# Tile-wise expert choice, split last output product and pre-weighted expert rows in a hybrid MoE layer

## The reference

```python
g_val, g_idx = lax.top_k(g_logits, 1)
...
e_val, e_idx = lax.top_k(e_in, TOP_K)
w_sel = jax.nn.softmax(e_val, axis=-1) * p_group
...
for e in range(N_EXPERTS):
    he = jax.nn.silu(h @ w_gate[e]) * (h @ w_up[e])
    y = y + combine[:, e:e + 1] * (he @ w_down[e])
```

## Time and profile before

| | |
|---|---|
| median of three runs | 708.25 us |
| the profiled execution | 710.35 us |
| its span | 708.4 us |
| TensorE busy | 693.4 us (98%) |
| VectorE busy | 294.6 us (42%) |
| HBM traffic over the span | 261 GB/s |

### The profile page before, as it was taken

The page is one execution under the profiler, slowest core; times in us unless marked ns, Lnnn a source line. Parts: engine busy times, 40 slices in busy tenths (PEclk is TensorE's granted clock), DMA queues, the critical chain, the costliest instruction groups (busy, mean ns, idle before and its releaser), DMA issues.

```text
span 708.4 us, 8000 instructions
## 1 busy us (share of the span) xinstructions
PE 693.4 (98%) x3274; PEld 417.6 (59%) x3274; DVE 294.6 (42%) x505; ACT 114.7 (16%) x199; POOL 180.9 (26%) x128
## 2 busy tenths in 40 slices
PE   9999999999999999999999999999999999999994
PEld 5444587555776457777877888647434434443431
DVE  3438492678320385744343324326413212212315
ACT  4111011111010422221122240013000000000004
POOL 0008989798369100710000000000000000000013
PEclk9999999999999999999999999998999999999997
DMA  8994536752433331533471235997999999999992
GB/s 354 420 396 186 183 145 237 297 201 96 179 114 124 118 115 33 209 120 118 176 297 61 76 148 207 426 392 296 374 418 421 420 423 420 421 420 421 418 408 81
DMA packets 29509, 183.70 MB, mean 259 GB/s; under 512 B 3543, under 2 KB 5975, under 8 KB 14624
## 3 DMA queue, kind: packets, MB, share of 16 engines
q1 hardware_dynamic: 27600, 178.98, 63.7%
q0 software_dynamic: 1584, 3.97, 1.4%
q10 hardware_dynamic: 288, 0.23, 0.1%
HBM read 178.14 MB, written 6.82 MB: 261 GB/s over the span
## 4 chain that ended last, share of the span: by engine, by line
PE 93%; DMA 2%; DVE 2%; POOL 1%; issue 0%; ACT 0%; DVEq 0%; POOLq 0%; ACTq 0%
PE bank L1183 21%; PE bank L798 18%; PE bank L802 10%; PE bank L794 8%; PE bank L815 6%; PE bank L1143 4%; PE bank L1021 4%; PE bank L821 4%; PE bank L946 2%; PE bank L967 2%; PE bank L844 2%; PE bank L808 2%; PE bank L954 2%; DMA y_rows<-sb,token_rows 1%; DMA sb<-y_rows 1%; PE bank L1000 1%
## 5 line engine op out<-in xcount | busy, mean ns | idle before, releaser
L1183 PE MATMUL bank<-sb 128*64 128x512 f32 x768 | 166.8, 593 | 0.7 <-ACT sb L729 0.7
L798 PE MATMUL bank<-sb 128*128 128x256 f32 x576 | 128.1, 381 | 0.0
L798 PEld LDWEIGHTS bank<-sb 128*128 128x128 f32 x576 | 108.2, 190 | 16.4 <-issue 2.4
L1183 PEld LDWEIGHTS bank<-sb 128*64 128x64 f32 x768 | 53.9, 137 | 106.9 <-issue 105.0
L584 POOL DMA_INDIRECT y_rows<-sb,token_rows x7 | 7.0, 1000 | 363.8 <-DVE sb L1740 363.8
L544 POOL TENSOR_TENSOR sb<-sb 128x1024 f32<-128x1024 f32 x32 | 66.8, 2089 | 55.6 <-DMA sb<-ada_w 36.0
L802 PE MATMUL bank<-sb 128*128 128x512 f32 x160 | 70.1, 593 | 0.0
L1372 DVE COPY sb<-bank 128x512 f32<-128x512 f32 x45 | 29.2, 685 | 96.4 <-PE bank L954 57.8
L794 PE MATMUL bank<-sb 128*128 128x512 f32 x128 | 55.8, 592 | 0.0
L802 PEld LDWEIGHTS bank<-sb 128*128 128x128 f32 x160 | 29.9, 190 | 34.7 <-issue 34.6
L1705 DVE TENSOR_TENSOR sb<-sb,bank 128x512 f32<-128x512 f32 x8 | 5.5, 688 | 97.1 <-PE bank L1183 97.1
(11 more groups left out here) (246 smaller groups left out, 689.8 us busy)
## 6 DMA issues: line engine op xcount, KB each, us to landing
sb<-expert_w SPq DMA_DIRECT2D x90, 1024.0 KB, 19.3
sb<-front_w SPq DMA_DIRECT2D x19, 2048.0 KB, 7.9
sb<-ada_w SPq DMA_DIRECT2D x32, 512.0 KB, 3.4
sb<-ada_mix SPq DMA_DIRECT2D x4, 2048.0 KB, 19.8
sb<-expert_w SPq DMA_DIRECT2D x12, 512.0 KB, 10.9
sb<-xcT SPq DMA_DIRECT2D x4, 512.0 KB, 6.3
sb<-front_w SPq DMA_DIRECT2D x4, 512.0 KB, 21.2
y_rows<-sb SPq DMA_DIRECT2D x4, 512.0 KB, 23.2
```

What stands on the lines that cost most here:

```text
L798: ins = pe.matmul(ps[:, c * L:(c + 1) * L], lhs(w, k, (2 * i + c) * P), hT[:, k, 0:L], start=(k == 0), stop=(k == KD - 1))
L1183: ins = pe.matmul(bank[e * CAP:(e + 1) * CAP, :], lhsT[:, k, e * CAP:(e + 1) * CAP], weights_at(k, e), start=(k == 0), stop=(k == parts - 1))
```

## The change

- The (out0, t1) product is cut after four of eight steps, tile zero is turned in between, and tile zero's router products and choice (`choose`, now for one tile) come before the end of the last output product. That product is made in two halves of 256 columns in different banks; residual, turning and routing of its tokens follow half by half.
- Positions, the first pair's one-hot matrix and the first gather are made tile by tile; `keep_warm` goes.
- `modulate` counts up after each block; the first gate product waits for one block at a time.
- The weight of each choice lies beside the token number, so that the product that finds a slot's row also finds its weight; `experts_out` multiplies it in before the rows are stored. Reads back are then plain adds; the weights' part of `choices` and ScalarE's two multiplications go. GpSimd's own reads are the first and the last of the four.
- VectorE adds both its rows before the last y, and the first scatter product before it waits for GpSimd. The multiplication by the gain moves to GpSimd. ScalarE issues the last output store.

The core of the diff (buffers, semaphores and renamed counters left out):

```diff
-        token_of = keep(NT * NE, NT, NE)
+        token_weight = keep(2 * NT * NE, NT, 2 * NE)
+        token_of, comb = [token_weight.rearrange("p t (e k) -> p t e k", k=2)[:, :, :, k] for k in range(2)]
...
-            sp.wait_ge(fill_ready, multiplied("out1"))
+            sp.wait_ge(last_out, 1)
             load_both(9)
...
-            for i in (1, 0):
-                for t in range(NT):
-                    cols = slice(512 * i, 512 * i + 512)
-                    sp.wait_ge(fin_by["act" if i == 0 else "dve"], t + 1)
-                    sp.dma_start(d["out"][t * P:t * P + P, cols], normed[:, t, cols]).then_inc(stored, 16)
+                                             .rearrange("a p n -> p (a n)")).then_inc(pass_in[m], 16)
+            for t, i in ((0, 1), (0, 0), (1, 1)):
+                cols = slice(512 * i, 512 * i + 512)
+                sp.wait_ge(fin_by["act" if i == 0 else "dve"], t + 1)
+                sp.dma_start(d["out"][t * P:t * P + P, cols], normed[:, t, cols]).then_inc(stored, 16)
             sp.wait_ge(stored, 16 * 2 * NT)
...
-            for q in range(2 * NT):
+            for q in (1, 0, NT, NT + 1):
                 pool.dma_start(y_back[:, q, :], d["y_rows"][q * P:q * P + P, :]).then_inc(y_in[q], 16)
             pool.wait_ge(acc_ready, 1)
...
-                pool.wait_ge(rows_weighted, q // NT + 1)
+                pool.wait_ge(y_in[q], 16)
                 pool.tensor_tensor(acc[:, 1, :], acc[:, 1, :], y_back[:, q, :], ALU.add).then_inc(pool_rows, 1)
                 pool.wait_ge(pool_rows, q // NT + 1)
+            pool.wait_ge(glast_in, 16)
+            for t in range(NT):
+                pool.wait_ge(scat_out, t + 1)
+                pool.tensor_tensor(xg[:, t, :], acc[:, t, 0:512], g_last[:, 0:512], ALU.mult).then_inc(xg_ready, 1)
...
-                    act.wait_ge(x1_ready, u + 1)
+                    act.wait_ge(x1_ready, u + 1 + (u == 3))
...
-            act.wait_ge(acc_ready, 1)
-            for q in (1, NT + 1):
-                act.wait_ge(y_in[q], 16)
-                act.activation(y_back[:, q, :], y_back[:, q, :], ACT.Copy, scale=slot_w[:, q:q + 1]).then_inc(rows_weighted, 1)
...
+            act.wait_ge(fin_by["act"], NT)
+            act.dma_start(d["out"][P:2 * P, 0:512], normed[:, 1, 0:512]).then_inc(stored, 16)
...
+                if ks[-1] < KD - 1:
+                    return
...
-            for n in range(first_out, first_out + 3):
+            for n in range(first_out, first_out + 2):
                 fill(n)
+            fill(first_out + 2, range(0, 4))
             turn_tokens(0, 0)
             turn_tokens(0, 1)
-            fill(first_out + 3)
+            fill(first_out + 2, range(4, KD))
+            route(0, 0)
+            route(0, 1)
+            def last_columns(p):
+
+                n = first_out + 3
+                ps = (banks[BANK_OF[n]], score[0])[p]
+                if p == 0:
+                    wait_emptied(pe, max(m for m in range(n) if BANK_OF[m] == BANK_OF[n]))
+                w = slot[SLOT_OF[FRONT.index("out1")]]
+                for k in range(KD):
+                    ins = pe.matmul(ps[:, 0:256], yT[:, k, P:2 * P], w[:, k * 512 + 256 * p:k * 512 + 256 * p + 256],
+                                    start=(k == 0), stop=(k == KD - 1))
+                ins.then_inc((fill_ready, last_out)[p], 1)
+
...
+                pe.wait_ge(x1_ready, 4 + p)
+                if p:
+                    pe.wait_ge(xT_out["act"], 1)
+                else:
+                    pe.wait_ge(xT_out["dve"], 2)
+                for c in range(2):
+                    k = 4 + 2 * p + c
+                    ins = pe.transpose(shared[1 - p][:, c * P:(c + 1) * P], x_nat[:, 1, k * P:(k + 1) * P], ident)
...
+                pe.wait_ge(xT_out["dve"], 3 + p)
+                for c in (2 * p, 2 * p + 1):
+                    ins = pe.matmul(route_bank[1][:, 0:ROUTES], xT[1][1][:, c, :], sm("router")[:, 4 + c, 0:ROUTES],
+                                    start=False, stop=(c == 3))
...
+            last_columns(0)
             turn_tokens(1, 0)
-            route(0, 0)
-            turn_tokens(1, 1)
-            route(0, 1)
+            pe.wait_ge(member_ready, 1)
+            pe.matmul(pv_bank[:, 256:272], sm("upto"), member[:, 0, :], start=True, stop=True).then_inc(pos_ready, 1)
+            last_columns(1)
+            turn_last(0)
             route(1, 0)
-            route(1, 1)
+            turn_last(1)
+            route_last(0)
+            route_last(1)
             for i, g in enumerate(POOLED[LOOP_SUMS:]):
                 pe.wait_ge(ada_summed, LOOP_SUMS + i + 1)
                 pe.matmul(banks[4 + i][:, :], ones, ada_sum[g], start=True, stop=True).then_inc(row5_ready, 1)
-            keep_warm(2)
...
+                for i in range(2):
+                    for c in range(4):
+                        ins = pe.matmul(banks[i][:, c * P:(c + 1) * P], x_nat[:, t, (4 * i + c) * P:(4 * i + c + 1) * P],
+                                        S_now[0][:, t, :], start=(t == 0 and c == 0), stop=(t == NT - 1 and c == 3))
+                    if t == NT - 1:
+                        ins.then_inc(gather_ready, 1)
...
+            pe.wait_ge(xn_first, 1)
+            pe.wait_ge(first_cut, 1)
+            gather_first(0)
+            pe.wait_ge(member_ready, 2)
+            pe.matmul(pv_bank[:, 272:288], sm("upto"), member[:, 1, :], start=True, stop=False)
...
             ins.then_inc(pos_ready, 1)
-            pe.wait_ge(xn_ready, NT)
+            pe.wait_ge(xn_ready, 1)
+            pe.wait_ge(cut_ready, 1)
+            gather_first(1)
...
-                    pe.wait_ge(h_out, 2 * n)
...
+                pe.wait_ge(choice_ready, 1)
...
-                    ins = pe.matmul(banks[7][:, 384 + 2 * n:386 + 2 * n], S[:, t, :], token_of[:, t, 2 * n:2 * n + 2],
+                    ins = pe.matmul(banks[7][:, 384 + 4 * n:388 + 4 * n], S[:, t, :], token_weight[:, t, 4 * n:4 * n + 4],
...
-                    if n is not None and k % 4 == 0:
-                        pe.wait_ge(h_out, 2 * n + (k // 4 + 1))
+                    if n is not None and q == 0:
+                        pe.wait_ge(h_out, k + 1)
+                    elif n is not None and k % 4 == 0:
+                        pe.wait_ge(h_out, KD * n + (k + 4))
...
-            gather(0, S_now[0])
...
-            residual(first_out + 2)
...
-            tokens_out(1, 1)
-            rstd(1)
-            dve.wait_ge(const_ready, 1)
-            logits(0)
-            link(logits(1))
-
+            residual(first_out + 2)
...
+            def choose(t):
+
...
+                link(dve.tensor_reduce(r_gm[:, col], g, AX.X, ALU.max))
+                first_best(r_sel[:, t, :], g, r_gm[:, col], sm("rank")[:, NE - NG:NE], r_t[:, t, :], r_sm[:, col])
...
+                first_best(oh2[:, t, :], em, r_m2[:, col], sm("rank"), r_et[:, t, :], r_sm[:, col])
+                dve.tensor_tensor(member[:, t, :], oh1[:, t, :], oh2[:, t, :], ALU.add).then_inc(member_ready, 1)
...
+                link(dve.tensor_tensor(posm[:, t, :], pv_bank[:, 256 + NE * t:256 + NE * t + NE], member[:, t, :], ALU.mult))
...
+                return dve.tensor_tensor(S_now[0][:, t, :].rearrange("p (e c) -> p e c", c=CAP),
+                                         slots_iota.unsqueeze(1).broadcast_to([P, 2, CAP]),
+                                         posm[:, t, 0:2].unsqueeze(2).broadcast_to([P, 2, CAP]), ALU.is_equal)
...
+            dve.wait_ge(const_ready, 1)
+            link(logits(0))
+            choose(0)
+            dve.tensor_scalar(x_nat[:, 0, :], x_nat[:, 0, :], x1_inv[:, 0:1], None, ALU.mult).then_inc(xn_first, 1)
+            positions(0)
+            cut_first(0).then_inc(first_cut, 1)
+            for p in range(2):
+                cols = slice(512 + 256 * p, 768 + 256 * p)
+                if p == 0:
+                    dve.wait_ge(fill_ready, len(FILLS))
+                else:
+                    dve.wait_ge(last_out, 1)
+                ps = (banks[BANK_OF[first_out + 3]], score[0])[p]
+                link(dve.tensor_tensor(spare[:, 1, cols], ps[:, 0:256], row2[:, cols], ALU.mult))
+                dve.tensor_tensor(x_nat[:, 1, cols], x_nat[:, 1, cols], spare[:, 1, cols], ALU.add).then_inc(x1_ready, 1)
+            for p in range(2):
+                dve.wait_ge(xT_ready, 4 + p)
+                dve.tensor_copy(xT[1][1][:, 2 * p:2 * p + 2, :].rearrange("p a b -> p (a b)"), shared[1 - p][:, 0:256])\
+                   .then_inc(xT_out["dve"], 1)
+            rstd(1)
+            link(logits(1))
+            choose(1)
+            dve.tensor_tensor(r_eg, r_all[:, :, 0:NG], wide(r_gm, NG), ALU.subtract).then_inc(gexp_in, 1)
             dve.tensor_tensor(r_d, r_m2, r_m1, ALU.subtract).then_inc(gexp_in, 1)
-            first_best(oh2, r_em, r_m2, sm("rank"), r_et, r_sm, NE)
-            dve.tensor_tensor(member, oh1, oh2, ALU.add).then_inc(member_ready, 1)
+            positions(1)
```

(38 more changed lines are left out.)

109 lines of the change are left out of this document (52 added, 57 removed).

## The result

The changed kernel takes **703.93 us** (703.33 to 705.02, 4 runs); the kernel before took 708.26 beside it (708.22 to 709.32, 4 runs). The ratio on record is 0.9921, 95% interval 0.9905 to 0.9937; it is not the quotient of these two medians, which is 0.994. It is faster, as forecast. But 700.4 was forecast, and 703.93 lies 0.7 above the range of 699.0 to 703.2; applied to the median of 708.25 the ratio gives 702.7 (701.5 to 703.8), which lies inside it. The profiled execution took 704.13, its span is 702.1.

What follows compares the result with a forecast made beforehand. Bounds: TensorE, busy 179.30 of 180.30 us during the experts, and chains of waits either side. Front 3.6 plus tail 4.25 gave 7.85: execution 710.35 to 702.5, less 2.1 to the median, 700.4 us; range 699.0 to 703.2.

Steps and rivals of the forecast that it cites:

- the signs named for being right: Among them: first gate product near 489.9, last load landing near 684, 9 to 10 us from last down product to end.
- The front's term: Ahead of the experts: the first gate product starts at 489.9 instead of 493.52, 3.6 us earlier.
- half a microsecond before TensorE asks: In the front: tile zero's choice, 3.2 us from 472.9, is made at 476.3, before TensorE wants it at 476.8.
- The loads' term: Weight loads: ninth pair waits 2.6 us longer, ring places free 3.6 earlier, 7.6 us unused; loads end 3 us earlier.
- The tail's term: Behind the experts: from the last down product to the span's end 9.6 us instead of 13.85, a gain of 4.25.
- E: The end of the last down product, from which the tail is counted; forecast at 690.95.
- The offset to the median: Profiled execution 710.35 lay 2.1 us above the runs' median 708.25; the forecast took this off, 702.5 to 700.4.
- The half clock: Rival, front: TensorE again granted 1.2 GHz around row sums and gathers, 3.4 us lost, part hidden; 702.9 us, chance 0.15.
- The reads did not land late: Rival, tail: loads end no earlier than 687.3, stored rows are read late; 702.5 or 703.4 us, chance 0.13.
- The first choice was early enough: Rival, front: both choices stand in series behind the last output product, 3.2 us more; 703.6 us, chance 0.07.
- Starving of weights: Rival, loads: delayed loads make TensorE wait; slower only if the last lands after 695.3; 9 later gives 709.2; chance 0.05.
- The port lock: Tail: GpSimd and two-SBUF-input VectorE adds exclude each other; late reads then come to 703.4 us, without it 702.5.

Runs made afterwards that it cites:

- short_ends: Changed kernel with one instruction fewer in each tile's choice, and GpSimd instead of ScalarE scaling tile zero's left half at the end; 704.32 us, 0.9916 of the kernel before.
- loads_later: Changed kernel, but the ninth pair of loads and all behind it also wait for the end of the router products; 705.12 us, 0.9947 of the kernel before.
- lock_free: Changed kernel with the final gains loaded after the third read of stored rows, and VectorE's last y before its second row add; 704.66 us, 0.9922 of the kernel before.
- before_again: The kernel before, unchanged, run and profiled once more; 709.74 us, 0.9996 of the kernel before.
- late_choice: Changed kernel, but tile zero's choice, scaling and cut stand just ahead of tile one's choice on VectorE; 708.21 us, 0.9988 of the kernel before.
- tail_only: Kernel before plus only rows weighted before storing, plain adds, gain on GpSimd and last store from ScalarE; 707.22 us, 0.9960 of the kernel before.
- before_no_warm: Kernel before without its two warm-up products ahead of the position product; 711.45 us, 1.0017 of the kernel before.

## Why the prediction was right and wrong

**The mechanism held.** By the stages the gate starts 2.97 earlier, the weighting on ScalarE is out of the chain, the clock stays at 1.00, and TensorE waits for no load inside a pair. How much of the 2.97 is the clock's and how much the earlier choice's was not separated: no profile shows the kernel before without the half clock. Of the signs named for being right, the gate (490.63), the last load (685.5) and the tail (10.46) each came short.

**The front's term, 3.6, measured 2.97.** What failed is the price of a choice: "16, so 3.2". It took 3.61, since an instruction on one tile costs nearly as much as one on two (0.17 on 16 columns, 0.19 on 32), and those with a scalar for each partition 0.23 and not 0.2. Twice 0.4 had been missed. The second shows in full. The first ate the cover of "half a microsecond before TensorE asks": TensorE was ready at 476.69, the choice came at 476.71, and the second half started some 0.2 late, as short_ends gave it back. Against the sum's own marks that half still ended near 480.5, because the work ahead of it was a little cheaper than summed; but the router products behind it ended at 483.26 and not 482.9, so that the second choice started at 483.64, 0.4 after the sum's 483.2. TensorE's wait ahead of the second choice's product, 0.45, stayed under the 0.5 that I had set as the mark of an error.

**The loads' term failed as a step.** "There is room for the first to vanish in the second": 6.0 of the unused 7.6 us lay from 485.7 on, around and behind the gate's start, and the earlier gate uses them up (404 GB/s and not 302). The later ninth pair opens a new hole ahead of it, 2.9 us at 23 GB/s, with nothing unused behind to make it good. The last load came 1.8 earlier and not 3. loads_later shows such a delay at the end whole.

**The tail's term, 4.25, measured 3.39.** The last scattered add ended at E + 4.35 to the digit; it hangs on the scatter's end (695.27, E + 3.63). GpSimd's second add ended at 693.88, E + 2.2, before the E + 2.8 of the sum; its read landed at 691.08, which is E - 0.56, where the sum had E - 0.55 (690.4 against 690.95). That was partly luck: the reads and E were both late, by 0.7. The two terms that were mis-sized come later. The last root ends at 697.55, E + 5.9 and not E + 5.4: the sum put the last square right behind the last add, but ScalarE's other squares stand ahead of it. It starts 0.53 after the last add's end (695.99 to 696.52), and in the sum's own it had started 0.75 after it (701.26 to 702.01). VectorE's wait of 0.49 for GpSimd is not the whole cause, for in lock_free, without such a wait, the delay is 0.75 too (696.03 to 696.78). The last store takes 2.9, not the 2.5 taken from SP's stores.

**The offset to the median failed.** I took the execution's 2.1 us above the median along into the forecast, 702.5 to 700.4. The median of three was low, not the execution high, and by the clocks of before_again's group low because its runs most likely lacked the stretch at half clock. The sum of 3.6 is reckoned on a profile with that stretch, against row sums at the full clock; to take the offset off as well then counts the clock's loss twice. The profiled execution after, 704.13, is 0.2 above its median. Of the 3.5 that 703.93 lies above 700.4, this is 1.9, the two terms are 1.5 (7.85 less 6.36), and 0.1 is the stage's start.

**The rivals.** The half clock did not come in the changed kernel. That full-width work right behind the small kept it away is argued; in late_choice, where TensorE idled 1.53 and 0.77 for the choice, it came. tail_only and before_no_warm show what it costs on a gather, 1.6 us of front more than on the row sums. The reads did not land late against E, as told above; the chain runs through them all the same, with a wait of 0.49 on VectorE. The first choice was early enough but for 0.2. Starving of weights did not happen, with 2.6 us to spare, and loads_later shows that it would cost as the rival had it. The port lock, raised there as a danger of this order of adds, is real: it costs 0.9 as soon as the reads come 1.2 earlier.

## What to carry to other kernels

Cutting a chain of tiny instructions in two halves buys overlap, not shorter chains: count instructions, not elements, and see which half is still on the path. When a wait moves, ask where the queue behind it now stands idle; slack that the change itself uses up cannot hide a second delay. Before an instruction is placed right behind another engine's last one, look in the profile for what that engine still has queued. Do not carry the offset of one profiled execution against three runs into a forecast before asking what it consists of: here it was most likely the loss that the change removes, and the kernel before spread over 3.4 us, half of the gain.

## What the hardware showed that was not expected

- VectorE's smallest instructions in the choices took 0.16 to 0.24 us almost whatever their size: 0.17 on 16 columns with constants, 0.19 on 32, 0.23 on 4 or 16 with a scalar for each partition.
- The same stretch of about 6.85 us at 1.2 GHz cost 1.6 us more on a gather than on row sums under a choice. The work under it decides.
- The runs of one kernel parted by their mean granted clock: 708.1 to 708.7 us at 0.996 or more, 709.5 to 711.4 at 0.992 or less.
- GpSimd needed 2.04 us to scale 128x512 by a scalar beside VectorE (how much of it was waiting was not separated), and 1.25 (2.50 for two) to multiply two tensors of that size.
- A store from ScalarE's queue landed after 2.9 us behind three others, and after 2.0 in short_ends, where two of the others came later.
